# Expert stages: gathers in pairs with v rows eight rows later, signals per two rows, fourteen diagonals, and the top-16 choosing in steps between the dots

## What is computed

```python
def peer_ffn(h, wq, k1, k2, u_tab, v_tab):
    def block(xb):                                   # 128 positions
        q = (xb @ wq).reshape(PEER_BLOCK, PEER_HEADS, 2, PEER_HALF)
        s1 = jnp.einsum('phd,kd->phk', q[:, :, 0], k1)
        s2 = jnp.einsum('phd,kd->phk', q[:, :, 1], k2)
        v1, i1 = lax.top_k(s1, PEER_TOPK)
        v2, i2 = lax.top_k(s2, PEER_TOPK)
        cand = (v1[..., :, None] + v2[..., None, :])
        ...
        top_s, top_pos = lax.top_k(cand, PEER_TOPK)
        eid = jnp.take_along_axis(cand_id, top_pos, axis=-1)
        g = jax.nn.softmax(top_s, axis=-1)
        ue, ve = u_tab[eid], v_tab[eid]
        act = jax.nn.gelu(jnp.einsum('pd,phkd->phk', xb, ue))
        return jnp.einsum('phk,phkd->pd', g * act, ve)
```

## Time and profile before

| | us |
|---|---|
| median of 3 runs | 4218.69 (4210.43 to 4220.34) |
| the profiled execution | 4216.61 |
| its span, first to last instruction | 4214.3 |
| PE busy | 3466.7 (82%) |
| DVE busy | 2018.0 (48%) |
| POOL busy | 1014.8 (24%) |
| ACT busy | 920.2 (22%) |
| queue of the gathers | 147456 packets, 536.94 MB |
| first expert stage's gathers | from 272.9 to 1044.3 |
| second expert stage's gathers | from 1278.1 to 2051.3 |

### The profile page before, as it was taken

One profiled execution on the slowest core, in us unless ns is written; L12 is line 12 of the kernel. 1 busy time (PEld: TensorE's weight loads), 2 busy tenths in 40 slices (PEclk: granted clock), 3 DMA queues, 4 the chain that ended last, 5 costly groups with the idle time before them and its releaser, 6 DMA issues. The chain is left out here.

```text
span 4214.3 us, 34019 instructions
## 1 busy us (share of the span) xinstructions
PE 3466.7 (82%) x12104; PEld 2275.1 (54%) x12104; DVE 2018.0 (48%) x3540; ACT 920.2 (22%) x1477; POOL 1014.8 (24%) x1081
## 2 busy tenths in 40 slices
PE   5884777678885767777899798999898989999797
PEld 3662332223564223223487587877587868665386
DVE  5575555651536656554343554532544445311354
ACT  0101111111111111111231333421343312201142
POOL 0025666665004666666200000000000000200000
PEclk9797888889887888888999899999999989999899
DMA  9468999998718899999554154554255534243353
GB/s 350 156 245 310 370 370 349 358 368 318 277 62 319 331 344 370 356 367 373 187 190 152 60 180 156 187 161 140 70 187 161 187 130 140 71 160 118 120 171 109
DMA packets 402035, 951.13 MB, mean 226 GB/s; under 512 B 30652, under 2 KB 171488, under 8 KB 401632
## 3 DMA queue, kind: packets, MB, share of 16 engines
q0 software_dynamic: 147456, 536.94, 33.7%
q1 hardware_dynamic: 245088, 397.09, 28.3%
q10 hardware_dynamic: 9344, 15.22, 1.0%
HBM read 948.06 MB, written 1.07 MB: 225 GB/s over the span
## 5 line engine op out<-in xcount | busy, mean ns | idle before, releaser
L1306 PE MATMUL PS<-v_rows,xn 128*128 128x512 f32 x2048 | 1042.4, 669 | 351.3 <-DMA v_rows<-in_peer_v_dram,peer_ids 303.7
L1306 PEld LDWEIGHTS PS<-v_rows,xn 128*128 128x128 f32 x2048 | 428.9, 215 | 963.8 <-issue 944.3
L1357 DVE CUSTOM_DVE_ANT_0 u_rows<-u_rows,PS 128x1024 f32<-128x1024 f32 x512 | 608.9, 1219 | 395.3 <-DMA u_rows<-in_peer_u_dram,peer_ids 339.2
L687 DVE TENSOR_TENSOR ring_lo<-ring,ring_hi 128x2048 fp32r<-128x2048 f32 x198 | 452.2, 2291 | 275.0 <-ACT ring_hi L642 275.0
L1407 POOL DMA_INDIRECT v_rows<-in_peer_v_dram,peer_ids x512 | 483.8, 945 | 363.7 <-PE PS L1306 203.0
L1407 POOL DMA_INDIRECT u_rows<-in_peer_u_dram,peer_ids x512 | 481.6, 941 | 297.7 <-issue 156.6
L439 PE MATMUL PS<-hT,ring 128*128 128x256 f32 x2048 | 450.3, 382 | 5.0 <-DVE hT L405 2.3
L642 ACT CAST ring_hi<-ring 128x2048 fp32r<-128x2048 f32 x198 | 375.2, 1904 | 319.3 <-PE PS L557 165.0
L557 PE MATMUL PS<-ring_hi,hT_hi 128*128 128x512 f32 x1056 | 423.0, 401 | 19.7 <-DVE hT_lo L710 19.7
L1345 ACT ACTIVATE xn<-cst,xn 128x128 f32<-128x128 f32 x512 | 189.9, 397 | 1092.0 <-PE PS L1306 663.5
L439 PEld LDWEIGHTS PS<-hT,ring 128*128 128x128 f32 x2048 | 391.5, 192 | 61.7 <-issue 5.3
(11 more groups left out here) (356 smaller groups left out, 2793.7 us busy)
## 6 DMA issues: line engine op xcount, KB each, us to landing
ring<-in_ffn_w_gate_dram SPq DMA_DIRECT2D x132, 512.0 KB, 4.0
...
```

The source lines that it names most:

```text
L687: nc.vector.tensor_tensor(halves(c)[1], slot, halves(c)[0], ALU.subtract).then_inc(S.w_lo, 1)
L1306: ins = nc.tensor.matmul(self.PS[:, 2 * b + h, :], diag[:, n % NDIAG, :], rowsV[:, m % VRING, h * BANK:(h + 1) * BANK], start=first, stop= ...
L1357: nc.vector.tensor_tensor_reduce(rowsU[:, m % URING, :], rowsU[:, m % URING, :], H[b], 1.0, 0.0, ALU.mult, ALU.add, dots[:, e:e + 1]).then ...
```

## The change

Sizes: `URING` 12 to 10, `VRING` 8 to 10, `NDIAG` 6 to 14, `GROUP` gone, `VLAG` = 4 new. POOL issues two u gathers and two v gathers in turn, the v pair 20 pairs (40 rows) behind the u pair. `u_used`, `v_used` and `S.diag` count pairs of rows. The top-16 functions become generators: each `yield` ends a step, and `products(p, ahead)` takes one step of `choose(p + 1)` after each dot. Only `choose(0)` stands ahead of the dots. `gates` moves to four rows before a part's end, and the product with gelu (`weigh`) into the next part, after its second dot. ACT makes the first two exponentials only after all four collections, and the later ones after a part's last diagonal. `acc` moves into the memory of the queries, and dots, weights and diagonals fill both halves of `xn`. The first block's residual comes after part 5 in place of after part 4, counted from 0.

```diff
-URING = 12
-VRING = 8
-GROUP = 4
-NDIAG = 6
+URING = 10
+VRING = 10
+NDIAG = 14
+VLAG = 4
...
                         nc.vector.max(values[:, i, c], src[:, i, :])
                     nc.vector.drain()
+                    yield
                     for i in range(n):
                         nc.vector.max_index(indices[:, i, c], values[:, i, c], src[:, i, :])
                     nc.vector.drain()
+                    yield
                     if half == 0:
                         for i in range(n):
                             nc.vector.match_replace(src[:, i, :], values[:, i, c], src[:, i, :], TAKEN)
                         nc.vector.drain()
+                        yield
...
-                top16(v16, i16, SC[:, b, LISTS * q:LISTS * (q + 1)], LISTS)
+                yield from top16(v16, i16, SC[:, b, LISTS * q:LISTS * (q + 1)], LISTS)
...
                 nc.vector.drain()
+                yield
...
-                top16(ts, tp, cand, PAIR)
+                yield from top16(ts, tp, cand, PAIR)
                 if count > 1:
                     ve.wait_ge(S.expd, count - 1)
...
                 nc.vector.drain()
+                yield
...
                     nc.vector.drain()
+                    yield
                     nc.vector.tensor_tensor(pick[:], pick[:], idx[:, s].unsqueeze(2).to_broadcast(full), ALU.mult)
                     nc.vector.drain()
+                    yield
                     nc.vector.tensor_reduce(found[:, s], pick[:], AX.X, ALU.add)
                     nc.vector.drain()
+                    yield
...
-                acc = self.xn[:, 0, :]
-                dots, wts = self.xn[:, 1, 0:P], self.xn[:, 1, P:2 * P]
-                diag = self.xn[:, 1, 2 * P:].rearrange("p (d n) -> p d n", n=P)
+                acc = QT[:, 0].rearrange("p t n -> p (t n)")
+                spare = self.xn[:].rearrange("p b d -> p (b d)")
+                dots, wts = spare[:, 0:P], spare[:, P:2 * P]
+                diag = spare[:, 2 * P:].rearrange("p (d n) -> p d n", n=P)
...
-                        p, i = n // PICKS, n % PICKS
-                        b, m = work[p][0], l * slots + n
+                        b, m = work[n // PICKS][0], l * slots + n
                         first, last = n % (slots // NB) == 0, n % (slots // NB) == slots // NB - 1
-                        pe.wait_ge(S.diag, n + 1)
+                        if n % 2 == 0:
+                            pe.wait_ge(S.diag, n // 2 + 1)
                         pe.wait_ge(*slot_landed(self.v_landed, VRING, m))
                         for h in range(2):
                             ins = nc.tensor.matmul(self.PS[:, 2 * b + h, :], diag[:, n % NDIAG, :],
                                                    rowsV[:, m % VRING, h * BANK:(h + 1) * BANK],
                                                    start=first, stop=last, skip_group_check=True)
-                        ins.then_inc(self.v_used, 1)
+                        if n % 2 == 1:
+                            ins.then_inc(self.v_used, 1)
...
-                        if 1 <= j <= 2:
-                            exponentials(act, S, *work[j - 1], j)
+                    for p in range(2):
+                        exponentials(act, S, *work[p], p + 1)
...
-                            if n >= NDIAG:
-                                act.wait_ge(self.v_used, l * slots + n - NDIAG + 1)
-                            nc.scalar.activation(diag[:, n % NDIAG, :], self.ident, ACT.Copy, scale=wts[:, e:e + 1]).then_inc(S.diag, 1)
-                            if i == PICKS // 2 and p + 2 < len(work):
-                                exponentials(act, S, *work[p + 2], p + 3)
+                            if n >= NDIAG and n % 2 == 0:
+                                act.wait_ge(self.v_used, (l * slots + n + 2 - NDIAG) // 2)
+                            ins = nc.scalar.activation(diag[:, n % NDIAG, :], self.ident, ACT.Copy, scale=wts[:, e:e + 1])
+                            if n % 2 == 1:
+                                ins.then_inc(S.diag, 1)
+                        if p + 2 < len(work):
+                            exponentials(act, S, *work[p + 2], p + 3)
...
-                    def products(p):
-
-                        b = work[p][0]
+                    def weigh(p):
+
+                        c = slice(PICKS * work[p][1], PICKS * (work[p][1] + 1))
+                        ve.wait_ge(S.gelu, p + 1)
+                        nc.vector.tensor_tensor(wts[:, c], wts[:, c], G[:, work[p][0], c], ALU.mult)
+                        nc.vector.drain().then_inc(S.weights, 1)
+
+                    def products(p, ahead):
+
+                        b, q = work[p]
                         for i in range(PICKS):
                             m, e = l * slots + p * PICKS + i, expert(p, i)
                             ve.wait_ge(*slot_landed(self.u_landed, URING, m))
-                            nc.vector.tensor_tensor_reduce(rowsU[:, m % URING, :], rowsU[:, m % URING, :], H[b], 1.0, 0.0, ALU.mult,
-                                                           ALU.add, dots[:, e:e + 1]).then_inc(self.u_used, 1)
+                            ins = nc.vector.tensor_tensor_reduce(rowsU[:, m % URING, :], rowsU[:, m % URING, :], H[b], 1.0, 0.0, ALU.mult,
+                                                                 ALU.add, dots[:, e:e + 1])
+                            if i % 2 == 1:
+                                ins.then_inc(self.u_used, 1)
+                            if i == 1 and p > 0:
+                                weigh(p - 1)
+                            if i == PICKS - 4:
+                                gates(ve, S, b, q, p + 1)
+                            next(ahead, None)
                         nc.vector.drain().then_inc(S.dots, 1)
 
                     def choose(p):
 
                         b, q = work[p]
                         ve.wait_ge(S.score_out, 2 * q + b + 1)
-                        lists(b, q)
-                        pairs(ve, S, b, q, p + 1)
+                        yield from lists(b, q)
+                        yield from pairs(ve, S, b, q, p + 1)
...
                     self.norm_vector(ve, S, self.modA[:, 1, :], shift)
                     ve.wait_ge(S.keysT, 1)
                     nc.vector.tensor_copy(keysT[:].rearrange("p i n -> p (i n)"), self.PS[:, 3, 0:2 * P]).then_inc(S.keysT_out, 1)
-                    choose(0)
-                    choose(1)
+                    for _ in choose(0):
+                        pass
                     for p, (b, q) in enumerate(work):
                         if q == 0:
                             ve.wait_ge(S.back, b + 1)
-                        products(p)
-                        gates(ve, S, b, q, p + 1)
-                        c = slice(PICKS * q, PICKS * (q + 1))
-                        ve.wait_ge(S.gelu, p + 1)
-                        nc.vector.tensor_tensor(wts[:, c], wts[:, c], G[:, b, c], ALU.mult)
-                        nc.vector.drain().then_inc(S.weights, 1)
-                        if p + 2 < len(work):
-                            choose(p + 2)
-                        if p not in (parts, len(work) - 1):
-                            continue
-                        done = 0 if p == parts else 1
-                        ve.wait_ge(self.v_used, l * slots + (done + 1) * slots // NB)
-                        nc.vector.tensor_tensor(acc.rearrange("p (h n) -> p h n", h=2), self.PS[:, 2 * done:2 * done + 2, :],
-                                                self.gate[:, 1, :].rearrange("p (h n) -> p h n", h=2), ALU.mult)
-                        nc.vector.drain()
-                        nc.vector.tensor_tensor(self.X[:, done, :], self.X[:, done, :], acc, ALU.add)
-                        nc.vector.drain()
+                        products(p, choose(p + 1) if p + 1 < len(work) else iter(()))
+                        if p == parts + 1:
+                            residual(0)
+                    weigh(len(work) - 1)
+                    residual(1)
 
...
-                        if m + GROUP > ring:
-                            pool.wait_ge(used, m + GROUP - ring)
-                        for i in range(GROUP):
-                            e = expert(p, first + i)
+                        m = l * slots + n
+                        if m + 2 > ring:
+                            pool.wait_ge(used, (m + 2 - ring) // 2)
+                        for i in range(2):
+                            e = expert(n // PICKS, n % PICKS + i)
...
-                    pool.wait_ge(S.ids, 1)
-                    for first in range(0, PICKS, GROUP):
-                        gather(0, first, 0)
-                    for p in range(len(work)):
-                        if p + 1 < len(work):
-                            pool.wait_ge(S.ids, p + 2)
-                        for first in range(0, PICKS, GROUP):
-                            if p + 1 < len(work):
-                                gather(p + 1, first, 0)
```

(9 more changed lines are left out.)

12 lines of the change are left out of this document (9 added, 3 removed).

## The result

The changed kernel takes 4183.8 us (median of 6 runs, 4179.5 to 4195.1) against 4214.1 us of the kernel before beside it (4209.5 to 4220.3): a ratio of 0.9933, 95% interval 0.9917 to 0.9949. That is 30 us, about half of the 57 to 62 us forecast. The profiled execution took 4192.7 us, with a span of 4190.9.

What follows compares the result with a forecast made beforehand. Bound: POOL stopping at used-up rings while completions are held. Head to 380, middle 564, tail 79 give 1023 against 1054.1 us, 62 us won over two stages: 4157 us (forecast 4130 to 4185; full range 4068 to 4228).

Steps and rivals of the forecast that it cites:

- What bounds the stage: Expert stages: no engine; POOL stops when a ring is used up, since PE and DVE completions are held during gather runs.
- Head: Stage start: fourth collection and first exponential done at 316 us, 67 gathers out at 380 where before 56.
- Tail: After the last u gather, bound by PE: 46 rows x 1.72 = 79 us, costing 7.5 us a stage.
- Middle: Between head and tail: runs grow from 24 to about 28 gathers, pause stays 4.4 us; 403 x 1.40 = 564 us.
- Its evidence: Support for 1.40 us a gather: the old middle's last 140 us, without choosing, had 100 gathers.
- the slack of 6 and 14 us: Middle: spare time for v slots to be freed and refilled, some 6 us before the change, 14 us after.
- Rival 1: Middle: completions late by only some 8 us, covered by v slack; 1.28 to 1.33 us a gather, 4077 us; chance 0.24.
- Rival 2: Ring of ten u rows stops POOL as often as choosing did, head late (321); about 4205 us; chance 0.17.
- Rival 3: Middle: DVE becomes the bound, its choosing steps held inside gather runs; slower, 4319 us; chance 0.13.
- The skill's rule: By it PE would never be held and rival 1's sum would apply; the prediction held the trace against it.

Runs made afterwards that it cites:

- e18: e4 with tiny matmuls and dots that read no gathered rows, POOL waiting in both rings only for landed gathers; output not computed; 4231.7 us.
- e5: Changed kernel, but before each pair POOL waits until the gather issued fourth before it has landed; 4315 us, ratio 1.0248.
- e12: e4 with v rows 32 behind u rows in place of 40 (VLAG 0); ratio 0.9915 to the kernel before.
- e4: Changed kernel with the old head: choosing of parts 0 and 1 ahead of the first dots, their exponentials between the collections; ratio 0.9884.
- e16: e4 with rings of 12 u and 8 v rows and each choosing in one piece behind a part's dots, two parts ahead; ratio 0.9981.
- e7: e4 without the choosing of parts 2 to 7, which reuse part 1's ids; output not computed; ratio 0.9848 to the kernel before.
- e3: Changed kernel with the next part's choosing in one piece behind a part's second dot, not in steps; ratio 1.0361.

## Why the prediction was right and wrong

- **What bounds the stage**: right in the main. POOL waits for news of freed slots, and the news is held beside a run of gathers (e18 and e5 show it from the two sides). "Only the stop brings the news that rows are free" was too strong: of the changed kernel's 43 drains that were held for over 2 us, 29 came free inside a run of POOL's, and in e12 ACT picks up the held projection at 337.99, in a run that POOL issued until 341.5.
- **Head**: right in its terms. Forecast 316 for the exponentials, measured 316.1; POOL's first long stop at 307, measured 309.4; 67 gathers at 380, measured 64. What I did not ask was whether the head without its reordering would be better still. It is, by 8 gathers (e4), since the later v rows already removed the hole of the earlier trace rows (e16 against e12, above).
- **Tail**: forecast 79 us, measured 79.9 and 83.1.
- **Middle**: here the forecast failed, in the step from longer runs to a better rate, "28 x 1.243 + 4.4 = 39.2 us, 1.40 us a gather". 403 x 1.40 = 564 us was the sum; measured are 405 gathers in 578.6 us and 406 in 575.5, or 1.43 and 1.42 each, at the upper end of the 1.37 to 1.44 that the forecast allowed. The runs did grow, but the pause grew with them. From 506.8 to 956.5 us the first middle is eleven runs of 24 to 32 gathers and nothing else, 28.7 on average: the run that was forecast. The pause behind them is 5.2 us on average, 4.9 without the usual gap of 0.3 that the 1.243 already holds, where the sum has 4.4, and a gather takes 1.423 us. At 32 gathers it is 5.5 to 5.9 us, and 6.0 in e7. Ahead of 506.8 short runs of 2 to 14 stand between the long ones, and 89 gathers take 1.45 us each. In all there were 17 stops of about 4.6 us, and not 14: 17 x (4.6 - 0.3) = 73 us are nearly all of the 75 beyond 405 x 1.243 = 503. The second middle has 18 stops of 4.0 us on average, and 5.1 us behind its last eight long runs. So a longer run gained next to nothing: without the gap the pause comes to 0.18 us a gather behind runs of 24 (median 4.6 us, the kernel before), and to 0.18 and 0.16 behind runs of 28 and 32 (5.2 and 5.5 us, the changed kernel).
- **Its evidence**: I chose 1.40 since the last 140 us of the middle before, free of choosing, had 100 gathers. The same stretch after has 96, and the kernel before has 98 in the second stage, 1.43 us each, which I left out:

```profile
1847.00:1987.00 140.00, 103.02 (x196) 42.28 (x196) 62.28 (x106) 21.20 (x55) 90.65 (x98) 0.87 0.96 366
```

What I read as freedom from choosing is the rate that runs of 24 have anyway. The pause of 4.07 us in the earlier trace rows was also a short one: behind the 18 runs of 24 gathers in the two middles before the median is 4.6. And the landing of 6.3 us "when the line is free" is that of the fifth gather behind a pause, with four others ahead of it; the slack of 6 and 14 us that is worked out from it rests on that misreading.
- **Rival 1** (the rings outlast the hold-up) came about in no kernel: the lowest rate is 1.41. **Rival 2** had the nearer total, 4205 with 10 rows of u blamed, but not the reason: stops for dots fell to 8.1 us. Rival 3's mechanism is real in e3 alone. The held drains did rise, from 137 to 253 us, but e7 shows them to cost at most a few us a stage here.
- **The skill's rule** that a DMA is not slowed by a compute operation "and vice versa" (Trainium skill, SBUF — State Buffer, "SBUF: two separate sides") holds here for the instructions themselves: the 512 dots of the kernel before take 1205 to 1223 ns each. It says nothing of completions, and these are what is held: steps of 0.9 us take 9.0 beside a full line in e18, and a window of 4 gathers removes it (e5). So a held drain was no evidence against the rule, and the rule was no ground for rival 1.

What stays open: why every kernel whose slots are freed by PE or DVE ends between 1.41 and 1.45 us per gather once its line is kept busy (e3 and e5 apart), with 3 stops or 23, at paces from 1.24 to 1.41. The parts are measured (signals are held beside a full line; behind stops of over 3 us the line moves 295 GB/s in its first 12 us in the kernel before and 285 in the changed one), and they offset each other, but no run shows that they must. It is open, too, whether the line's load or POOL's issuing delays the signals, and what ends a hold: at POOL's restarts the line is mostly near its end (a median of 45 KB moves in the 0.9 us after them in the changed kernel), but in e4's head ACT is released at 333.57 with the line still at 426 GB/s. Which path the signals share with the transfers wasn't tried either.
